# Residual additions and the first units of the next layer by halves of the tokens, squares added by GpSimd

## The reference

```
def rmsnorm(x, g):
    y = xf * lax.rsqrt(jnp.mean(xf * xf, axis=-1, keepdims=True) + EPS)
    return y * g
...
        x = x + rmsnorm(y, norm_mix_post[l])      # residual 1
        h = rmsnorm(x, norm_ffn_pre[l])
        y = conv_mlp(h, w_up[l], conv_ffn[l], w_down[l])
        x = x + rmsnorm(y, norm_ffn_post[l])      # residual 2
...
    proj = h @ w_in                               # latent attention: h = rms_norm(x, g) again
```

## Time and profile before

| | |
|---|---|
| median of 3 executions | 2005.63 us (2005.27 to 2011.18) |
| the profiled execution, its own time | 2007.84 us |
| its span, first to last instruction | 2006.0 us |
| PE busy | 1852.6 us (92%) |
| DVE busy | 1217.0 us (61%) |
| ACT busy | 529.2 us (26%) |
| POOL busy | 788.0 us (39%) |
| granted TensorE clock, mean | 0.967 |
| residual 1, first scaling to last `hl` | 516.87 to 566.08 us |
| residual 2, the same | 1295.95 to 1347.96 us |

### The profile page before, as it was taken

The page is one execution under the profiler, slowest core; times in us unless marked ns, Lnnn a source line. Parts: engine busy times, 40 slices in busy tenths (PEclk is TensorE's granted clock), DMA queues, the critical chain, the costliest instruction groups (busy, mean ns, idle before and its releaser), DMA issues.

```text
span 2006.0 us, 21677 instructions
## 1 busy us (share of the span) xinstructions
PE 1852.6 (92%) x8508; PEld 1516.6 (76%) x8508; DVE 1217.0 (61%) x1112; ACT 529.2 (26%) x608; POOL 788.0 (39%) x321
## 2 busy tenths in 40 slices
PE   6999994789787999999999999779989999999996
PEld 5887884678576888888888888557878888888785
DVE  6106537871778567655665567686546666666634
ACT  4005002321331000000000000231236566665522
POOL 5444555215463443544354445546431010101042
PEclk9998997789898999999999999989999999999998
DMA  4222112111321111211111102142221010101232
GB/s 156 110 98 95 53 42 84 43 42 63 126 84 36 49 47 38 63 42 52 31 63 42 52 31 65 72 157 64 74 95 37 32 42 32 42 31 63 79 116 84
DMA packets 39836, 131.78 MB, mean 66 GB/s; under 512 B 4544, under 2 KB 4928, under 8 KB 39776
## 3 DMA queue, kind: packets, MB, share of 16 engines
q1 hardware_dynamic: 22128, 78.13, 12.3%
q10 hardware_dynamic: 17648, 52.80, 7.2%
HBM read 104.18 MB, written 26.74 MB: 65 GB/s over the span
## 4 chain that ended last, share of the span: by engine, by line
PE 76%; DVE 16%; issue 4%; ACT 3%; POOL 1%; DMA 1%; DVEq 0%; ACTq 0%; POOLq 0%
PE psum L422 50%; PE psum L762 5%; PE psum L783 4%; PE psum L720 4%; PE psum L819 4%; PE psum L772 2%; DVE cc L1554 2%; DVE spv L1448 2%; PE psum L745 1%; DVE yo L1520 1%; DVE rstd L1295 1%; PE psum L663 1%; DVE ptl L1668 1%; DVE uu L1304 1%; ACT pth L1171 1%
## 5 line engine op out<-in xcount | busy, mean ns | idle before, releaser
L324 POOL TENSOR_TENSOR wh<-wstage,ones 128x1024 fp32r<-128x1024 f32 x133 | 334.3, 2513 | 1021.1 <-PE psum L422 627.0
L422 PE MATMUL psum<-hh,wh 128*128 128x512 f32 x1316 | 412.1, 395 | 52.6 <-DVE hl L1299 20.9
L422 PE MATMUL psum<-hl,wh 128*128 128x512 f32 x1316 | 409.3, 392 | 0.0
L422 PE MATMUL psum<-hh,wl 128*128 128x512 f32 x1316 | 408.5, 392 | 0.0
L327 POOL TENSOR_TENSOR wl<-wstage,wh 128x1024 fp32r<-128x1024 f32 x133 | 356.2, 2678 | 10.4
L422 PEld LDWEIGHTS psum<-hh,wh 128*128 128x128 f32 x1316 | 248.1, 190 | 113.1 <-issue 32.9
L422 PEld LDWEIGHTS psum<-hh,wl 128*128 128x128 f32 x1316 | 249.3, 189 | 52.5
L422 PEld LDWEIGHTS psum<-hl,wh 128*128 128x128 f32 x1316 | 249.2, 189 | 52.4
L1554 DVE SCALAR_TENSOR_TENSOR cc<-uu,col,cc 128x1023 f32<-128x1023 f32 x88 | 182.5, 2074 | 10.5 <-DVE cc L1548 0.8
L1304 DVE TENSOR_TENSOR uu<-psum,rstd 128x1024 f32<-128x1024 f32 x44 | 53.7, 1222 | 142.7 <-PE psum L422 142.6
L1574 DVE TENSOR_TENSOR yo<-yo,psum 128x1024 f32<-128x1024 f32 x80 | 97.4, 1217 | 57.1 <-PE psum L422 57.1
(11 more groups left out here) (280 smaller groups left out, 3041.7 us busy)
## 6 DMA issues: line engine op xcount, KB each, us to landing
wstage<-w_units SPq DMA_DIRECT2D x133, 512.0 KB, 3.4
resid<-yo ACTq DMA_DIRECT2D x16, 512.0 KB, 2.9
mix<-spill ACTq DMA_DIRECT2D x12, 512.0 KB, 2.6
xin<-xT ACTq DMA_DIRECT2D x8, 512.0 KB, 8.4
xr<-xT ACTq DMA_DIRECT2D x8, 512.0 KB, 4.3
xr<-resid ACTq DMA_DIRECT2D x8, 512.0 KB, 4.2
gates<-gspill ACTq DMA_DIRECT2D x8, 512.0 KB, 2.6
rstd<-gates ACTq DMA_DIRECT2D x16, 256.0 KB, 3.0
```

The costliest lines, as they stand in the source:

```text
L324: pool.tensor_tensor(wh[:, slot_], wstage[:, s], ones[:, :].unsqueeze(1).to_broadcast([P, 8, P]), ALU.mult).then_inc(w_high, 1)
L422: mm = pe.matmul(out[:, t], w[:, wslot, b, :], x[part][:, xk, t], start=start and n == 0, stop=stop and n == 2)
```

## The change

Both residuals now go over the first half of the tokens for all eight tiles, and then over the second. With them:

- PE (`units_by_halves`) does the first three units of the stage for one half, then for the other. After each half it forms that half's sum in bank 6 or 7. The fourth unit follows in these two banks, by halves.
- GpSimd adds the squares of tiles 1 to 6 of a half to `root`, six additions of 128x512 each, 12 in a residual where there were 7 of 128x1024. The square of tile 7 is added by PE, as a second matmul into the same bank.
- ACT no longer issues the DMAs of the residual. SyncE does, 16 stores and 12 loads of 128x512 in each residual, between its loads of weights: those up to unit 37 are issued ahead of residual 1, those up to 103 ahead of residual 2.
- Four units have to be split when a residual begins, so there is another place: `wx`, four tiles in a region that is free at these times. Unit 34 goes to the first half of `wx`. Units 100 and 101 go to both halves, and GpSimd splits them right after unit 99, ahead of its squares; 102 and 103 are split where 100 and 101 were. From unit 37 to 99 the ring is used with a shift of two.
- The reciprocals of the norm are taken by halves after the residual.

The core of the diff:

```diff
...
+            split_into(U_FF + 1, EXTRA[0], U_OUT + 1)
+            split_into(U_FF + 2, in_slot(1), U_FF - 1)
+            split_into(U_FF + 3, in_slot(2), U_FF)
             add_tiles(1)
...
+            pool.wait_ge(a_lo, 22)
+            for j in range(2):
+                split_into(U_L0 + 1 + j, EXTRA[j], None)
...
-            for u in range(U_L0 + 1, U_L0 + RING):
+            for u in range(U_L0 + 3, U_L0 + 5):
+                split_into(u, in_slot(u % RING), U_L0)
+            add_tiles(2)
...
             def add_tiles(n):
 
-                for k in range(1, KT):
-                    pool.wait_ge(sq_ready, n * KT + k + 1)
-                    pool.tensor_tensor(root[:, :], root[:, :], sq[:, k % 2, :], ALU.add).then_inc(sq_used, 1)
-                    pool.wait_ge(sq_used, n * (KT - 1) + k)
+                for half in range(2):
+                    t = slice(half * HT, half * HT + HT)
+                    for k in range(1, KT - 1):
+                        done = KT - 1 + (2 * n - 2 + half) * (KT - 2) + k - 1
+                        pool.wait_ge(sq_ready, KT + halves_before(n, half) + k + 1)
+                        pool.wait_ge(sq_used, done)
+                        pool.tensor_tensor(root[:, t], root[:, t], sq[:, k % 2, t], ALU.add).then_inc(sq_used, 1)
...
+            def units_by_halves(n, base, places, free):
+
+                for half in range(2):
+                    t = slice(half * HT, half * HT + HT)
+                    for k in range(KT):
+                        pe.wait_ge(h_lo, KT + halves_before(n, half) + k + 1)
+                        for j in range(3):
...
+                            mm = half_products(bank(2 * j + half), places[j], k, half, k == 0, k == KT - 1)
+                            if half and k == KT - 1:
+                                mm.then_inc(unit_done, 1)
+                    pe.wait_ge(sq_used, KT - 1 + (2 * n - 1 + half) * (KT - 2))
+                    pe.matmul(bank(6 + half), ones[:, :], root[:, t], start=True, stop=False)
+                    pe.wait_ge(sq_ready, KT + halves_before(n, half) + KT)
+                    pe.matmul(bank(6 + half), ones[:, :], sq[:, (KT - 1) % 2, t], start=False,
+                              stop=True).then_inc(norm_sum, 1)
+                pe.wait_ge(w_split, base + 4)
+                for half in range(2):
+                    pe.wait_ge(root_ready, 2 * n + half)
+                    for k in range(KT):
+                        mm = half_products(bank(6 + half), places[3], k, half, k == 0, k == KT - 1)
+                mm.then_inc(unit_done, 1)
...
+            def residual(n, source, dest):
+
+                for half in range(2):
+                    t = slice(half * HT, half * HT + HT)
+                    for k in range(KT):
+                        sync.wait_ge(res_ready, halves_before(n, half) + k + 1)
+                        sync.dma_start(dest[k, :, t], yo[:, k, t]).then_inc(res_out, DMA)
+                        if k + 2 < KT:
+                            sync.dma_start(xr[:, k % 2, t], source[k + 2, :, t]).then_inc(xr_in[k % 2][half], DMA)
...
+                    if half or n == 1:
+                        half_inverse(half, 2 * n - 1 + half)
+                    dve.wait_ge(half_rstd, 2 * n - 1 + half)
+                    for k in range(KT):
+                        dve.scalar_tensor_tensor(yo[:, k, t], yo[:, k, t], col[:, post + k:post + k + 1],
+                                                 rstd[:, t], ALU.mult, ALU.mult).then_inc(res_scaled, 1)
+                        if k:
+                            low(k - 1)
+                        dve.wait_ge(res_scaled, before + k + 1)
+                        dve.wait_ge(xr_in[k % 2][half], DMA * (4 * (n - 1) + k // 2 + 1))
+                        dve.tensor_tensor(yo[:, k, t], yo[:, k, t], xr[:, k % 2, t], ALU.add).then_inc(res_ready, 1)
+                    low(KT - 1)
+                for half in range(2):
+                    t = slice(half * HT, half * HT + HT)
+                    dve.wait_ge(root_ready, 2 * n + half)
+                    dve.reciprocal(rstd[:, t], root[:, t]).then_inc(rstd_ready, 1)
...
```

More of the change, by code:

```diff
@@ L293, in _ @@
                 sync.dma_start(sgo[:, :], mix[(3 * h + 2) * P:(3 * h + 3) * P, :]).then_inc(g_in, DMA)
-            with sync.Fori(before, main) as i:
+            def residual(n, source, dest):
[6 more added lines that the diff above has]
+                            sync.dma_start(xr[:, k % 2, t], source[k + 2, :, t]).then_inc(xr_in[k % 2][half], DMA)
+            first, second = (U_FF + 3) // STG, (U_L0 + 3) // STG
+            with sync.Fori(before, first) as i:
+                pairs_of_loads(i)
+            residual(1, xT, resid1)
+            with sync.Fori(first, second) as i:
+                pairs_of_loads(i)
+            residual(2, resid1, resid2)
+            with sync.Fori(second, main) as i:
                 pairs_of_loads(i)
@@ L318, in _, with split @@
             pool.wait_ge(m01_set, 3)
-            def split(u, s, slot_, loaded, used):
+            def split(u, s, place, loaded, used):
+                high, low = place
                 pool.wait_ge(w_loaded[s], loaded)
@@ L398, in _ @@
                                        ALU.mult).then_inc(acc_step2, 1)
[L399 removed]
+            for u in range(U_L0 + 3, U_L0 + 5):
+                split_into(u, in_slot(u % RING), U_L0)
+            add_tiles(2)
+            for u in range(U_L0 + 5, (U_L0 // 6 + 2) * 6):
                 split_one(u)
[L401 to L402 removed]
+            with pool.Fori(U_L0 // 6 + 2, NU // 6) as i:
                 split_six(i)
@@ L429, in unit, with first_units @@
                 mm.then_inc(unit_done, 1)
[L431 to L445, removed]
+            def first_units(wslots):
+                for k in range(KT):
+                    pe.wait_ge(h_lo, k + 1)
                     for j, wslot in enumerate(wslots):
@@ L618, in _, with down @@
             sum_half(1, 7, (acc_step, KT - 1), (evac, 37))
[L621 to L628, removed]
+            units_by_halves(1, U_FF, (in_slot(0), EXTRA[0], in_slot(1), in_slot(2)), (evac, 37))
+            def down(base, buf, groups, wslot=(U_LOOP + 6) % RING):
                 pe.wait_ge(w_split, base + 2)
@@ L1011, in _, with first_residuals @@
             output_high(HEADS - 1)
-            for k in range(2):
-                act.dma_start(xr[:, k, :], xT[k]).then_inc(xr_in[k], DMA)
+            def first_residuals(source):
+                for half in range(2):
+                    t = slice(half * HT, half * HT + HT)
+                    for k in range(2):
+                        act.dma_start(xr[:, k, t], source[k, :, t]).then_inc(xr_in[k][half], DMA)
+            first_residuals(xT)
             def out_tile(m, b):
@@ L1035, in _, with residual, norm_root @@
                 half_roots(half, 6 + half, half + 1)
[L1037 to L1050, removed]
-                        high_and_square(yo[:, k, :], gain, n, k)
-                act.wait_ge(norm_sum, n + 1)
-                take_root(root[:, :], slot(3), D, 0, root_ready)
-            residual(1, C_FPRE, xT, resid1)
-            act.wait_ge(h_lo, 2 * KT)
-            act.wait_ge(res_out, KT * DMA)
+            def residual(n, gain):
+                def norm_root(half):
+                    act.wait_ge(norm_sum, 2 * n + half)
+                    take_root(root[:, half * HT:half * HT + HT], bank(6 + half), D, 0, root_ready)
+                for half in range(2):
+                    t = slice(half * HT, half * HT + HT)
+                    for k in range(KT):
+                        act.wait_ge(res_ready, halves_before(n, half) + k + 1)
+                        high_and_square(yo[:, k, t], gain, k, t, KT - 1 + (2 * n - 2 + half) * (KT - 2))
+                        if half and k == 1:
+                            norm_root(0)
+                norm_root(1)
+            residual(1, C_FPRE)
+            act.wait_ge(h_lo, 3 * KT)
+            act.wait_ge(res_out, 2 * KT * DMA)
             for k in range(KT):
@@ L1086, in _ @@
                 ff_group(i, 1, False)
-            act.wait_ge(res_out, KT * DMA)
-            for k in range(2):
-                act.dma_start(xr[:, k, :], resid1[k]).then_inc(xr_in[k], DMA)
+            act.wait_ge(res_out, 2 * KT * DMA)
+            first_residuals(resid1)
             for half in range(2):
```

127 lines of the change are left out of this document (58 added, 69 removed).

## The result

The changed kernel takes **2013.58 us** in the median (18 runs, 2010.66 to 2017.19), the kernel before, run beside it, 2006.96 (18 runs): a ratio of 1.0032, 95% interval 1.0025 to 1.0039, or 6.5 us slower. The forecast was 2003.7, some 2 us faster; it had the direction wrong, and the time lies just above its range.

What follows compares the result with a forecast made beforehand. The prediction took DVE to bound residual 1 and PE's restart residual 2; -4.2 and +2.3 us sum to -1.9, 2005.9 profiled, 2003.7 median. Its own range was 1999 to 2009, 8-in-10 1997 to 2013.

Steps and rivals of the forecast that it cites:

- the wait for ACT's high part: Residual 1 on DVE: low parts wait up to 0.15 us for each of 16 half tiles, 2.4, taken as 2.0.
- The other four terms of residual 1: On DVE: 16 half tiles 30.9 us, reciprocal 3.3, the split 2.9, GpSimd's twelve additions 12.9.
- In residual 2: On DVE: 30.9 + 3.3 + 12.9 + 2.0 plus splits of 102 and 103, 7.5; sum 56.6 us, +4.6.
- The price of an addition: In the residuals, each half-wide GpSimd addition holds DVE 1.08 us, half of 2.15; 12.9 a residual.
- The rival of the whole instruction: Each of 24 GpSimd additions costs DVE 1.28 us, and PE has no slack at the down products: 2011.0, chance 0.11.
- the 2012.9 of the loads: Rival: residual loads set the pace, taking 5.5 us each and adding 9.2 us: 2012.9, chance 0.07.
- The rival by which GpSimd's additions fall into DVE's wait for ACT: GpSimd costs less: additions give back 3.6 us of waits, and DVE gains 3.6 between splits: 1996.5, chance 0.20.
- Tails and splits: Residual 1's tail 8.0 us, -8.3, with GpSimd's splits +1.3 by unit 37; residual 2's tail 3.9, -5.9.
- The down products: Ahead of residual 2, new splits hold DVE's additions of squares 6.1 us, less PE's slack of 2.5: +3.6.
- The loads: Half-tile loads in the residuals, taken at 3.7 us, hide behind DVE's work and cost nothing.

Runs made afterwards that it cites:

- Experiment 5: The changed kernel with DVE's scalings issued one tile earlier, GpSimd still adding the squares: 2006.16 us, ratio 0.9992 to the kernel before.
- Experiment 4: The changed kernel with splits of 100 and 101 behind the second half's squares, 102 and 103 behind the residual's squares: 2011.24 us, ratio 1.0015 to before.
- experiments 1: The changed kernel without GpSimd's 24 additions of squares in the two residuals: 1987.52 us, ratio 0.9903 to the kernel before.
- Experiments 2: The changed kernel with DVE adding the squares in place of GpSimd, one behind each residual addition: 1996.5 us, ratio 0.9941 to the kernel before.
- 6: The changed kernel with DVE adding squares, splits of 100 and 101 behind the second half's squares, 102 and 103 after the last low part: 1992.18 us.
- 7: The changed kernel with DVE adding squares, late splits of 100 to 103, and unit 36's split between the halves of residual 1: 1989.85 us.
- experiment 3: The kernel before, at full width, with DVE adding the squares in both residuals in place of GpSimd: 1995.74 us, ratio 0.9942 to the kernel before.

## Why the prediction was wrong

**The step that failed is the wait for ACT's high part,** "2.4; the additions of squares cover some of that, I take 2.0". It failed twice. 0.2 us was lost at each of seven tiles of a half, 2.8 in all, rather than 0.15 or less; and the eighth tile has no next scaling behind it, so its low part waits 0.79, twice a residual. Together that is 4.4, not 2.0. And GpSimd's additions cover none of it: they start when ACT's square is done, 0.1 us before DVE's low part gives way to the next addition (530.25 and 530.36), and so fall on that addition each time. The other four terms of residual 1 give 50.0 (30.9 + 3.3 + 2.9 + 12.9), with 4.4 it is 54.4 against a measured 55.4. Counted from start to start the term is 4.9: the eighth low part stands 2.57 us behind its addition (540.08 to 542.65), of which 1.09 is GpSimd's and 0.60 the plain spacing, so 0.88 is the wait, and the first addition of a half, with no low part ahead of it, starts 0.78 behind its own scaling (546.70 to 547.48) rather than 0.66: 2.9 + 1.8 + 0.2. The last 0.5 is spread over the additions (12 x 1.09 = 13.1) and rounding. In residual 2 likewise 54.6 + 4.4 = 59.0 against 60.0. So 3.4 us in each residual were missed, 2.4 to 2.9 of them in this term. Experiment 5 bears it out: with the wait out of the chain the residuals are 5.2 and 4.9 shorter.

**The price of an addition was right,** in part by luck. Half of 2.15 gave 1.08, and the row of 527.12 shows 1.78 - 0.69 = 1.09. What does not hold DVE is not half as long, though: of the 2.77 at 543.21 the first 0.43 lie ahead of the held instruction and the last 0.19 behind its hold, of the 1.33 at 527.01 it is 0.11 and 0.13. The rival of the whole instruction would have had every one cost 1.28; they last 1.33 in the kernel. The Trainium skill (SBUF — State Buffer, SBUF: two separate sides) has the two engines exclude each other for the whole instruction. The trace agrees to within 0.24 us: DVE's held addition ends at 528.90, and less its own 0.69 that is 528.21, while GpSimd's instruction runs from 527.01 to 528.34. Its first 0.11 us lies ahead of the held addition's start, beside DVE's low part, and its last 0.13 no longer holds. That rival's 2011.0 and the 2012.9 of the loads were the nearest to the time, both for reasons that were not there. The first of them also had PE's clock down at the down products: it was granted 1.00 there (1280 to 1287), as in residual 1 from 528 to 543 and from 560 to 571, so PE was not the bound there either. The rival by which GpSimd's additions fall into DVE's wait for ACT fails on the rows above: the wait is over at 529.69, GpSimd starts at 530.25.

**Tails and splits were right:** 8.25 and 4.1 us against 8.0 and 3.9, unit 37 +1.4 against +1.3. The gain of 14 us in two tails is there in full.

**The down products** were right in kind, DVE held by each of four instructions of GpSimd and PE through its bank, and 1.25 short in size: +4.85 against +3.6. The slack of PE of 2.5 us was used up after step 7, and three gaps of 1.1 us followed. Experiment 4 takes all of it back.

**The loads** hid, as forecast. Those of residual 1 landed in

```profile
DMA to landing us min/median/max: 2.6/3.1/3.4
```

less than the 3.7 I had taken. They show as soon as the residual gets faster (experiments 1 and 5).

**Not foreseen,** and in favour of the profiled execution of after: PE's wait of 2.58 us at 1462.12 is not in it. The change did not take that wait away. Experiments 2, 4, 6 and 7, which are by halves too, have it (2.57 or 2.58), as has experiment 3 at full width; 1 and 5 do not. It hangs on who goes first where DVE comes 0.3 us behind a split, and that came out either way with the same 0.3 us; nothing in the traces ties it to the change, so it counts as luck. Without it the two profiled executions would differ by 6.2 us rather than 3.4. How the executions behind the medians fell is not known, since no other was traced.

By terms: 3.7 missed in residual 1, 4.8 in residual 2 with its down products, 0.6 elsewhere, less 2.8, is 6.3, from -1.9 to the +4.4 that the two profiled executions show from the first scaling on. The medians say +6.5, which lies between this +4.4 and the +7.2 that the same rows give without the -2.8.

**What the forecast never asked** is the larger point: whether the additions belonged on GpSimd at all. It had both numbers, 2.15 for what one takes from DVE and 1.14 for an addition of that size on DVE, and never set them beside each other. The change kept the additions on GpSimd and turned seven wide ones into twelve narrow ones, which cost DVE 13 us a residual where doing them itself costs 7.

## What to carry to other kernels

Work that is moved to GpSimd is not off DVE's path if both use SBUF with two inputs: set what its instruction takes from DVE (here 0.8 of its length) beside what DVE would need itself, and if DVE is the bound, give GpSimd what falls beside reciprocals and reads of PSUM. When a chain through several engines is cut into halves, each link's length is what must be covered; look for the last tile, which has no successor to cover it, and try the order with one step more of distance. A tail that gets shorter pays only where its shortening is not spent again on the loop in front of it.

## What the runs showed of the hardware

- A GpSimd addition of 128x512 in fp32, 1.33 us long, takes 1.09 us from a DVE instruction with two SBUF inputs beside it; one of 128x1024, 2.77 long, takes 2.15. DVE does the same additions in 0.60 and 1.14.
- Beside splits that follow one another, DVE got one instruction with two SBUF inputs through for each instruction of GpSimd: in the rows from 1273.83 on, each addition of squares takes 2.29, each addition from PSUM 0.68.
- The engine whose row starts first is not always the one that goes first: with DVE 0.3 us behind a split, three DVE instructions took 7.87 us at 1436.46 of the kernel before, and 3.49 at 1442.10 of after, where the split took 6.05 instead of 2.62.
- A reciprocal of 128x512 takes 3.35 us beside a split (534.66 in experiment 7) and alone (543.32 in after), so a split costs nothing there.
